# A mixture-of-experts loop whose 2 MB weight blocks come over one queue: the blocks of the second matrix are issued from ScalarE instead

## The chip, the cores and the metric

The kernel runs on one core of a Trainium2 chip. The metric is the device time of one execution in microseconds (us). The median of three executions of the kernel before is 1500.68 us (1499.49 to 1815.03). The profiled execution, from which all rows below come, took 1503.03 us, of which its span is 1501.1 us.

## What is computed

One layer of a hybrid backbone on 256 latent and 256 context tokens of width 1024, in float32: a token mixer (three kinds of scans), then a mixture of 32 experts of which each token uses four. This case is about the mixture:

```python
for e in range(N_EXPERTS):                       # 32
    gu = t @ p['moe_w_gu'][e] + p['moe_b_gu'][e]     # (256, 1024) @ (1024, 2048)
    glu, lin = jnp.split(gu, 2, axis=-1)
    glu = jnp.minimum(glu, SWIGLU_LIMIT)
    lin = jnp.clip(lin, -SWIGLU_LIMIT, SWIGLU_LIMIT)
    act = glu * jax.nn.sigmoid(SWIGLU_ALPHA * glu) * (lin + 1.0)
    y = y + gates[:, e:e + 1] * (act @ p['moe_w_down'][e] + p['moe_b_down'][e])   # (256, 1024) @ (1024, 1024)
```

The kernel computes, for each expert, only the (at most 64) tokens that chose it; an expert chosen by more gets an extra round behind the 32. All weights of all 32 experts are read whatever the routing: 32 x 6 blocks of 2 MB.

## The kernel before, in words

**Blocks and ring.** An expert's first matrix (`moe_w_gu`) comes as four blocks of 2 MB, its second (`moe_w_down`) as two. The text calls them U0 to U3 and D4, D5. All go through a ring of eight slots (`RING = 8`), filled in the order U0 U1 U2 U3 D4 D5 of expert 0, then of expert 1 and so on: block q goes to slot q mod 8. `ring_full[r]` counts landings in slot r, `ring_free[r]` how often TensorE is through with it. The loops are unrolled over groups of four experts (`GROUP`), since after four experts (24 blocks) the slots repeat.

**SyncE (SP) before.** SyncE issues every block in that order (line 605, in `load_slot`), each behind a wait for its slot (lines 610 and 629). The first eight have no earlier use of the slot to wait for: U0 to U3 of expert 0 come as soon as the mixer's output is there, D4 and D5 wait for the four slots in which `w_out` lay (`slot_free`), and the next two for steps of the router stage (`h2_ready`, the copies hk0 and hk1).

**TensorE (PE).** `expert(m, i, ...)` does, in this order: `up` (U0 to U3: two chunks of rows, k, to a block, four matmuls of 128x512 to a chunk, with a scatter of the expert before and the transposes `select_back` after chunk 0 and the bias after chunk 3), a second part of the scatter, `turn` of half 0, `gather` for an expert to come, `turn` of half 1, `down` (D4, then D5). A matmul in float32 is two instructions in the trace: 16 to an up block, 32 to `down`. `up` waits for `ring_full` of a block and gives its slot free behind its last matmul.

**VectorE (DVE).** When U3 is done (it waits for that slot's `ring_free`), the clamps L1707 and L1708, L1711, and L1714, which multiplies by the sigmoid; then the same for the second half. TensorE's turn (L2499) waits for L1714. Later L1734 takes down's result.

**ScalarE (ACT).** `expert` there: `copy_selT` (L1062, behind `select_back`), `sigmoid_half` 0 and 1 (L1052, each behind L1707's `glu_ready`), `copy_actT` (L1057) and `copy_gathered` (L1047). In the loop over groups (`Fori`) the first expert has two table loads (`ACT_TABLE_LOAD`), one ahead of L1062's copy and one ahead of the first L1052, since the table of the sigmoid is another than the copy's. The last group, written out behind the loop, has none ahead of its sigmoids.

Nothing in this kernel orders the blocks on the DMA engines except the order in which SyncE issues them: one queue, first in, first out.

Of the kernel before, what the change touches and what calls it, by code (L numbers as in the profile page):

```python
# [17 lines left out]
E, TOPK, FF, SLOTS = 32, 4, 1024, 64  # L18
EXTRA = L * TOPK // SLOTS
WORDS = 53152  # L20
RING = 8
PER = 6
GROUP = 4
# [214 lines left out]
def hybrid_block(nc, a):  # L238

    with ExitStack() as ctx:  # L240
# [198 lines left out]
        def pair(name, n=1024):  # L439

            g = R.group(name)
            return PS[:, 2 * g:2 * g + 2, :].rearrange("p a b -> p (a b)")[:, 0:n]
# [81 lines left out]
        def ring_at(m, i, s):  # L524

            q = PER * i + s
            return q % RING, m * 3 + q // RING

        def extra_at(j, s):

            return s, j + E * PER // RING
# [3 lines left out]
        @block.sync  # L535
        def _(sp):
            def slot_wait(kind, n):

                for s, count in before[kind, n]:
                    sp.wait_ge(slot_free[s], count)  # L540

            sp.dma_start(Cb(C_ID), a["consts"][:, 0:P]).then_inc(ident_in, 16)
            sp.dma_start(xtok[:, 0:2, :], a["ctx"][0].rearrange("(i p) d -> p i d", p=P)).then_inc(x_in, 16)
            sp.dma_start(xtok[:, 2:4, :], a["x"][0].rearrange("(i p) d -> p i d", p=P)).then_inc(x_in, 16)

            def load_ada(n):
                s = place["ada", n][0]
                slot_wait("ada", n)
                sp.dma_start(slots[s], w_ada_k[n % 8, :, n // 8 * 2048:n // 8 * 2048 + 2048]).then_inc(slot_full[s], 16)

            sp.dma_start(Cb(1, C_N - 1), a["consts"][:, P:]).then_inc(consts_in, 16)
            sp.wait_ge(rows_in, 16 * N_ROWS)
            for n in range(8):
                load_ada(n)


            sp.wait_ge(zeroed, 1)

            def mats(dst, src):
                sp.dma_start(dst, src).then_inc(mats_in, 16)  # L560

            def spread(dst, src):

                mats(dst, src.partition_broadcast(P))

            for d in range(2):
                spread(w0b[:, 256 * d:256 * d + 256], a["rw_w0"][0, d, :])
                spread(gbb[:, P * d:P * d + P], a["gla_gate_b"][0, d, :])
                spread(dtb[:, 8 * d:8 * d + 8], a["ssd_dt_bias"][0, d, :])
                spread(alog[:, 8 * d:8 * d + 8], a["ssd_a_log"][0, d, :])  # L570
                mats(W2A[32 * d:32 * d + 32, 256 * d:256 * d + 256], a["rw_w2"][0, d])
                mats(gwb[16 * d:16 * d + 16, P * d:P * d + P], a["gla_gate_w"][0, d])
            spread(rbb, a["router_b"][0])
            spread(dall, a["ssd_d"][0])
            mats(W2A[64:96, 0:256], a["rw_a2"][0])
            mats(g2w[0:64, :], a["rw_g2"][0])
            mats(dtw[:, :, :], a["w_in"][0].rearrange("(k p) c -> p k c", p=P)[:, :, DT0:DT0 + 16])
            mats(rtw[:, :, :], a["router_w"][0].rearrange("(k p) c -> p k c", p=P))

            for s, _, kind, n in loads[8:]:  # L580
                if kind == "in":
                    c0, w, _ = W_GROUPS[n]
                    slot_wait("in", n)
                    sp.dma_start(w_in_tile(n), w_in_k[:, :, c0:c0 + w]).then_inc(slot_full[s], 16)
                elif kind == "ada":
                    load_ada(n)
            sp.wait_ge(gla_done, 1)
            for n in range(4):
                if n == 2:
                    sp.wait_ge(rw_in, 8)  # L590
                s = place["out", n][0]
                slot_wait("out", n)
                sp.dma_start(slots[s].rearrange("p (k c) -> p k c", k=2), w_out_k[:, 2 * n:2 * n + 2, :])\
                    .then_inc(slot_full[s], 16)


            sp.wait_ge(cat_ready, 1)
            for x in range(2):
                sp.dma_start(bgrow[32 * x:32 * x + E, :], a["moe_b_gu"][0, :, FF * x:FF * x + FF]).then_inc(late_in, 16)
            sp.dma_start(bdn[0:E, 0:D], a["moe_b_down"][0]).then_inc(late_in, 16)  # L600

            def load_slot(r, e, s):

                src = gu_k[bass.ds(e, 1), s, :, :] if s < 4 else dn_k[bass.ds(e, 1), s - 4, :, :]
                sp.dma_start(ring[r], src.rearrange("a p c -> p (a c)")).then_inc(ring_full[r], 16)

            for q in range(PER * GROUP):
                r, used = q % RING, q // RING
                if used:
                    sp.wait_ge(ring_free[r], used)  # L610
                elif r in (4, 5):
                    for x in range(2):
                        sp.wait_ge(slot_free[2 * r - 6 + x], base[2 * r - 6 + x])
                elif r == 6:
                    R.emptied(sp, "n2")
                    sp.wait_ge(h2_ready, 1)
                    R.emptied(sp, "xk0")
                    R.emptied(sp, "xk1")
                elif r == 7:
                    R.arrived(sp, "m5")  # L620
                    R.arrived(sp, "fg")
                    R.emptied(sp, "hk0")
                    R.emptied(sp, "hk1")
                load_slot(r, q // PER, q % PER)
            with sp.Fori(1, E // GROUP) as m:
                for i in range(GROUP):
                    for s in range(PER):
                        r, used = ring_at(m, i, s)
                        sp.wait_ge(ring_free[r], used)
                        load_slot(r, m * GROUP + i, s)  # L630

            R.emptied(sp, "lst")
            extra = sp.value_load(ints[0:1, 0:1], min_val=0, max_val=EXTRA)
            with sp.If(extra > 0):
                with sp.Fori(0, extra) as j:
                    e = sp.value_load(ints[0:1, bass.ds(j + 8, 1)], min_val=0, max_val=E - 1)
                    for s in range(PER):
                        r, used = extra_at(j, s)
                        sp.wait_ge(ring_free[r], used)
                        load_slot(r, e, s)  # L640
            for i in range(2):
                sp.wait_ge(out_ready, i + 1)
                sp.dma_start(a["out"][0, i * P:(i + 1) * P, :], xk[:, i, :]).then_inc(out_done, 16)
            sp.wait_ge(out_done, 32)
# [99 lines left out]
        def _(act):  # L744
# [269 lines left out]
            R.drained("m5", act.copy(m5r[0:E, :], pair("m5")[0:E, :]))  # L1014
            R.arrived(act, "fg")
            R.drained("fg", act.copy(fgr, pair("fg")))
            R.emptied(act, "n2")
            act.activation(r2, r2, ACT.Sqrt).then_inc(root_ready, 1)
            act.activation(small[:, 44:45], small[:, 12:13], ACT.Exp)  # L1019
# [29 lines left out]
            def sigmoid_half(n, half):  # L1049

                act.wait_ge(glu_ready, n * 2 + (half + 1))
                act.activation(sgm[:, 256 * half:256 * half + 256], glu[:, 256 * half:256 * half + 256], ACT.Sigmoid, scale=ALPHA).then_inc(sig_ready, 1)  # L1052
# [6 lines left out]
            def copy_selT(n, buffer):  # L1059

                act.wait_ge(selT_done, n + 1)
                act.copy(SW[:, buffer, :], PS[:, 3, 0:L]).then_inc(sw_ready, 1)  # L1062

            def expert(m, i, gathers):

                n = m * GROUP + i
                copy_selT(n, i % 2)
                sigmoid_half(n, 0)
                sigmoid_half(n, 1)
                copy_actT(n, 0, PS[:, 3, 0:256])  # L1070
                if gathers:
                    copy_gathered(i % 2, n + 3, (i // 2 + 1) % 2, 2)
                copy_actT(n, 1, PS[:, 0, 0:256])

            def extra_expert(j):

                n = j + E
                act.wait_ge(gathered, j + (E + 1))
                act.copy(hg[:, 0, 0:4, :].rearrange("p k t -> p (k t)"), PS[:, 2, :]).then_inc(hg_ready, 1)
                copy_selT(n, 1)  # L1080
                sigmoid_half(n, 0)
                sigmoid_half(n, 1)
                copy_actT(n, 0, PS[:, 3, 0:256])
                copy_actT(n, 1, PS[:, 0, 0:256])
# [4 lines left out]
                for i in range(GROUP):  # L1089
                    expert(m, i, True)  # L1090
            for i in range(GROUP):
                expert(E // GROUP - 1, i, i < 2)
            R.emptied(act, "lst")
            extra = act.value_load(ints[0:1, 0:1], min_val=0, max_val=EXTRA)
            with act.If(extra > 0):
                with act.Fori(0, extra) as j:
                    extra_expert(j)
            act.activation(small[:, 44:45], small[:, 12:13], ACT.Sqrt)
            for i in range(2):
                act.wait_ge(scattered, i + 1)  # L1100
# [1510 lines left out]
```

## Time and profile before

| | |
|---|---|
| median of 3 executions | 1500.68 us |
| profiled execution | 1503.03 us, span 1501.1 us |
| TensorE busy | 1336.3 us (89%) |
| VectorE, ScalarE, GpSimd busy | 411.4, 227.3, 53.1 us |
| DMA queue q1 (all from SyncE) | 451.38 MB, 72.2% of 16 engines' span |
| DMA queue q10 (from ScalarE) | 276 packets, 0.08 MB |
| read from HBM | 450.40 MB |

The span has two parts. Up to about 575 us the mixer and the router run. From there to the end the 32 experts run, TensorE is in the nines in every one of the 40 slices, and the DMA engines move 424 to 429 GB/s in nearly all of them. In a row of the timeline the number ahead is the start in us, the second the duration, and the brackets say how long the engine was idle before it and what ended that. In a DMA row the last number is the time from issue to landing.

### The profile page before, as it was taken

To read this page: it belongs to the slowest core of one execution; us is meant where nothing else is said; L and a number is where in the kernel's file an instruction comes from. 1 tells how busy PE (TensorE), PEld (TensorE's weight loads), DVE (VectorE), ACT (ScalarE), POOL (GpSimd) and SP (SyncE) were. 2 spreads that over 40 slices of the span, in tenths; PEclk is the share of its full clock that TensorE was granted. 3 is DMA by queue.
4 is the path that set the end of the run, shared out by engine and by line. 5 is a ranking of instruction groups with operands and counts; after the bars stand their busy time and mean duration, and the time that the engine had idled before them with its cause. 6 is when DMAs were issued, how large, how long until landed. Compare 5 with 4: busy or idle time off the path is not lost.

```text
span 1501.1 us, 21678 instructions
## 1 busy us (share of the span) xinstructions
PE 1336.3 (89%) x9148; PEld 639.8 (43%) x9148; DVE 411.4 (27%) x959; ACT 227.3 (15%) x426; POOL 53.1 (4%) x84
## 2 busy tenths in 40 slices
PE   4999998644888979999999999999999999998997
PEld 2545546423878874333333333333333333333332
DVE  0131135487454442112112112112112112111211
ACT  2122103332232131001001001001001001000101
POOL 0000000043121000000000000000000000000000
PEclk8999999866899979999999999999999999999999
DMA  8536510000101197999999999999999999999995
GB/s 331 189 138 226 202 68 0 1 0 19 40 3 59 47 380 290 424 428 426 427 426 428 428 427 428 427 428 427 427 427 429 428 427 427 428 428 426 428 426 234
DMA packets 44886, 452.44 MB, mean 301 GB/s; under 512 B 6998, under 2 KB 10036, under 8 KB 17044
## 3 DMA queue, kind: packets, MB, share of 16 engines
q1 hardware_dynamic: 44544, 451.38, 72.2%
q8 instruction: 53, 0.87, 0.2%
q10 hardware_dynamic: 276, 0.08, 0.0%
q14 instruction: 13, 0.11, 0.0%
HBM read 450.40 MB, written 1.05 MB: 301 GB/s over the span
## 4 chain that ended last, share of the span: by engine, by line
PE 43%; DMA 16%; DVE 3%; issue 1%; ACT 1%; DVEq 0%; SPq 0%
PE PS L1786 42%; DMA arena<-in_moe_w_gu 16%; PE PS L2499 1%; DVE arena L1708 1%; DVE arena L1711 1%; DVE arena L1714 1%; PE PS L2490 1%; ACT arena L1026 0%; DVE arena L1707 0%; DVE arena L1614 0%; ACT arena L1101 0%; DVE arena L1779 0%; ACT L1019 0%; DVEq L240 0%; DVE arena L1643 0%
## 5 line engine op out<-in xcount | busy, mean ns | idle before, releaser
L1786 PE MATMUL PS<-arena 128*64 128x512 f32 (+11 forms) x8746 | 1282.1, 425 | 113.5 <-DVE arena L1410 23.7
L1786 PEld LDWEIGHTS PS<-arena 128*64 128x64 f32 (+7 forms) x8746 | 593.2, 152 | 750.5 <-issue 599.9
L1707 DVE TENSOR_SCALAR arena<-PS 128x256 f32<-128x256 f32 x64 | 38.6, 602 | 522.3 <-PE PS L1786 522.3
L1052 ACT ACTIVATE arena<-arena 128x256 f32<-128x256 f32 x64 | 26.7, 418 | 491.1 <-DVE arena L1707 491.1
L1734 DVE TENSOR_TENSOR arena<-PS,arena 128x512 f32<-128x512 f32 x32 | 22.1, 692 | 219.3 <-PE PS L1786 219.3
L1062 ACT COPY arena<-PS 128x256 f32<-128x256 f32 x32 | 11.9, 373 | 288.7 <-PE PS L2490 288.7
L2499 PE MATMUL PS<-arena 128*128 128x128 f32 x128 | 26.2, 286 | 29.9 <-DVE arena L1714 29.9
L1205 DVE SCALAR_TENSOR_TENSOR arena<-PS,arena 128x255 f32<-128x255 f32 (+5 forms) x68 | 32.7, 481 | 41.8 <-ACT arena L820 39.5
L1708 DVE TENSOR_SCALAR arena<-PS 128x256 f32<-128x256 f32 x64 | 39.0, 610 | 0.0
L2499 PEld LDWEIGHTS PS<-arena 128*128 128x128 f32 x128 | 14.5, 141 | 56.1 <-DVE arena L1714 30.8
L1711 DVE SCALAR_TENSOR_TENSOR arena<-arena 128x256 f32<-128x256 f32 x64 | 27.3, 426 | 2.8
L1714 DVE TENSOR_TENSOR arena<-arena 128x256 f32<-128x256 f32 x64 | 27.3, 426 | 2.2
L1047 ACT COPY arena<-PS 128x512 f32<-128x512 f32 x32 | 18.8, 587 | 46.1 <-PE PS L1786 46.1
L1057 ACT COPY arena<-PS 128x256 f32<-128x256 f32 x64 | 23.5, 368 | 5.6 <-PE PS L2499 5.6
L1477 DVE TENSOR_TENSOR arena<-arena,PS 128x256 f32<-128x256 f32 x40 | 16.9, 421 | 24.4 <-PE PS L1786 23.7
L1690 DVE TENSOR_SCALAR arena<-arena 128x128 f32<-128x128 f32 x64 | 19.1, 341 | 0.0
L1463 DVE COPY arena<-PS 128x512 f32<-128x512 f32 x16 | 11.0, 689 | 27.6 <-PE PS L1786 27.6
L2490 PEld LDWEIGHTS PS<-arena 128*128 128x128 f32 x64 | 6.5, 141 | 24.3 <-issue 24.3
L983 ACT COPY arena<-PS 128x512 f32<-128x512 f32 x16 | 9.4, 587 | 41.3 <-PE PS L1786 41.3
L674 POOL TENSOR_TENSOR arena<-arena 128x128 f32<-128x128 f32 x8 | 3.5, 443 | 320.6 <-DVE arena L1328 309.6
L1300 DVE TENSOR_SCALAR arena<-PS,arena 128x256 f32<-128x256 f32 (+1 forms) x32 | 11.1, 410 | 11.3 <-ACT arena L891 11.2
L2490 PE MATMUL PS<-arena 128*128 128x128 f32 x64 | 14.0, 301 | 0.0
(276 smaller groups left out, 464.0 us busy)
## 6 DMA issues: line engine op xcount, KB each, us to landing
arena<-in_moe_w_gu SPq DMA_DIRECT2D x128, 2048.0 KB, 26.5
arena<-in_moe_w_down SPq DMA_DIRECT2D x64, 2048.0 KB, 29.0
arena<-in_w_ada SPq DMA_DIRECT2D x24, 1024.0 KB, 7.4
arena<-in_w_in SPq DMA_DIRECT2D x5, 2048.0 KB, 9.2
arena<-in_w_out SPq DMA_DIRECT2D x4, 1024.0 KB, 6.7
arena<-in_w_in SPq DMA_DIRECT2D x1, 1664.0 KB, 6.9
arena<-in_consts SPq DMA_DIRECT2D x1, 1536.0 KB, 11.0
arena<-in_w_in SPq DMA_DIRECT2D x1, 1152.0 KB, 5.6
```

Of the source, the lines that this page charges most:

```text
L1052: act.activation(sgm[:, 256 * half:256 * half + 256], glu[:, 256 * half:256 * half + 256], ACT.Sigmoid, scale=ALPHA).then_inc(sig_ready, 1)
L1057: act.copy(actT[:, 2 * half:2 * half + 2].rearrange("p a b c -> p (a b c)"), src).then_inc(actT_ready, 1)
L1205: ins = dve.scalar_tensor_tensor(out=d_, in0=s_, scalar=wgt, in1=d_, op0=ALU.mult, op1=ALU.add)
L1690: ins = dve.tensor_scalar(selw[:, i, :, :], slot_ids.unsqueeze(1).to_broadcast([P, 2, SLOTS]), pos(i), gates[:, i, bass.ds(e, 1)], ALU.is_ ...
L1707: dve.tensor_scalar(by_rest(glu), of_half(0), LIMIT, None, ALU.min).then_inc(glu_ready, 1)
L1708: dve.tensor_scalar(by_rest(lin), of_half(1), LIMIT, -LIMIT, ALU.min, ALU.max).then_inc(moe_vec, 1)
L1711: dve.scalar_tensor_tensor(out=lin[:, cols], in0=lin[:, cols], scalar=1.0, in1=glu[:, cols], op0=ALU.add, op1=ALU.mult).then_inc(moe_vec, 1)
L1714: dve.tensor_tensor(act_[:, cols], lin[:, cols], sgm[:, cols], ALU.mult).then_inc(act_ready, 1)
L1734: dve.tensor_tensor(ye, PS[:, 3, :], m5h, ALU.mult).then_inc(ye_ready, 1)
L1786: ins = pe.matmul(out, lhsT, rhs, start=start, stop=stop, skip_group_check=skip)
L2490: ins = pe.transpose(PS[:, 3, t * P:t * P + P], selw[:, t, :, :].rearrange("p a b -> p (a b)"), ident)
L2499: ins = pe.transpose(dst[:, c * P:c * P + P], act_[:, (2 * half + c) * P:(2 * half + c + 1) * P], ident)
```

## The change

`load_slot` on SyncE becomes `load_up`, which issues U0 to U3 only. D4 and D5 are issued by ScalarE (`load_down`): those of expert 0 behind the copies of m5 and fg, ahead of the n2 step; those of expert n+1 inside expert n, behind `copy_selT` and ahead of the sigmoids. Slots, sizes, semaphores and the waits for them stay.

```diff
-            def load_slot(r, e, s):
+            def load_up(r, e, s):
-                src = gu_k[bass.ds(e, 1), s, :, :] if s < 4 else dn_k[bass.ds(e, 1), s - 4, :, :]
-                sp.dma_start(ring[r], src.rearrange("a p c -> p (a c)")).then_inc(ring_full[r], 16)
+                sp.dma_start(ring[r], gu_k[bass.ds(e, 1), s, :, :].rearrange("a p c -> p (a c)")).then_inc(ring_full[r], 16)
...
             with sp.Fori(1, E // GROUP) as m:
                 for i in range(GROUP):
-                    for s in range(PER):
+                    for s in range(4):
                         r, used = ring_at(m, i, s)
                         sp.wait_ge(ring_free[r], used)
-                        load_slot(r, m * GROUP + i, s)
+                        load_up(r, m * GROUP + i, s)
...
             R.drained("fg", act.copy(fgr, pair("fg")))
+            def load_down(r, e, s):
+                act.dma_start(ring[r], dn_k[bass.ds(e, 1), s - 4, :, :].rearrange("a p c -> p (a c)")).then_inc(ring_full[r], 16)
+            for s in (4, 5):
+                for x in range(2):
+                    act.wait_ge(slot_free[2 * s - 6 + x], base[2 * s - 6 + x])
+                load_down(s, 0, s)
             R.emptied(act, "n2")
...
-            def expert(m, i, gathers):
+            def load_next(m, i):
+                for s in (4, 5):
+                    r, used = ring_at(m + (i + 1) // GROUP, (i + 1) % GROUP, s)
+                    act.wait_ge(ring_free[r], used)
+                    load_down(r, m * GROUP + (i + 1), s)
+            def expert(m, i, gathers, more=True):
                 n = m * GROUP + i
                 copy_selT(n, i % 2)
+                if more:
+                    load_next(m, i)
                 sigmoid_half(n, 0)
```

The last expert issues nothing (`more` is false). The extra rounds are changed in the same way.

SyncE's program at the first blocks of the ring, before (the brackets name the semaphores that a row waits for):

```order
L605 DMA arena<-in_moe_w_gu 128x4096 x4
L605 DMA arena<-in_moe_w_down 128x4096 [waits slot_free3,slot_free2]
L605 DMA arena<-in_moe_w_down 128x4096 [waits slot_free5,slot_free4]
L605 DMA arena<-in_moe_w_gu 128x4096 [waits pair_free0,pair_free1,h2_ready,pair_free3]
L605 DMA arena<-in_moe_w_gu 128x4096 [waits pair_free3,pair_free0,pair_full2,pair_full1]
L605 DMA arena<-in_moe_w_gu 128x4096 [waits ring_free0]
L605 DMA arena<-in_moe_w_gu 128x4096 [waits ring_free1]
L605 DMA arena<-in_moe_w_down 128x4096 [waits ring_free2]
L605 DMA arena<-in_moe_w_down 128x4096 [waits ring_free3]
```

and in the change:

```order
L604 DMA arena<-in_moe_w_gu 128x4096 x4
L604 DMA arena<-in_moe_w_gu 128x4096 [waits pair_free0,pair_free1,h2_ready,pair_free3]
L604 DMA arena<-in_moe_w_gu 128x4096 [waits pair_free3,pair_free0,pair_full2,pair_full1]
L604 DMA arena<-in_moe_w_gu 128x4096 [waits ring_free0]
L604 DMA arena<-in_moe_w_gu 128x4096 [waits ring_free1]
L604 DMA arena<-in_moe_w_gu 128x4096 [waits ring_free4]
L604 DMA arena<-in_moe_w_gu 128x4096 [waits ring_free5]
```

The four rows of the second matrix have left SyncE's program; the others keep their waits.

ScalarE's program at the first expert of the loop over groups, before (L1062 is copy_selT, L1052 the sigmoid, ISA and REGISTER_ALU work on addresses and counts):

```order
L1062 ACT_TABLE_LOAD
L1062 COPY arena<-PS 128x256 [waits selT_done]
L1051 ISA
L1052 ACT_TABLE_LOAD
L1052 ACTIVATE arena<-arena 128x256 [waits glu_ready]
L1051 REGISTER_ALU
L1052 ACTIVATE arena<-arena 128x256 [waits glu_ready]
L1057 COPY arena<-PS 128x256 [waits actT_done]
```

and in the change, where L1069 is copy_selT, L1018 the DMA and L1059 the sigmoid:

```order
L1069 ACT_TABLE_LOAD
L1069 COPY arena<-PS 128x256 [waits selT_done]
L1075 ISA
L1018 ISA [waits ring_free2]
L1018 DMA arena<-in_moe_w_down 128x4096
L1018 ISA [waits ring_free3]
L1018 DMA arena<-in_moe_w_down 128x4096
L1058 ISA
L1059 ACT_TABLE_LOAD
L1059 ACTIVATE arena<-arena 128x256 [waits glu_ready]
L1058 REGISTER_ALU
L1059 ACTIVATE arena<-arena 128x256 [waits glu_ready]
```

Two waits and two issues now stand between the copy and the sigmoid, and the sigmoid's table load stands behind them.

## Rows read from the trace of the kernel before

**Rows 1.** Page, part 2: GB/s in 40 slices of 37.5 us

```profile
GB/s 331 189 138 226 202 68 0 1 0 19 40 3 59 47 380 290 424 428 426 427 426 428 428 427 428 427 428 427 427 427 429 428 427 427 428 428 426 428 426 234
```

**Rows 2.** Chain that ended last, pieces: start us, us, what

```profile
704.83 1.79 PE PS L1786 x16
...
732.92 1.79 PE PS L1786 x16
...
1087.27 32.71 DMA arena<-in_moe_w_gu
...
1143.91 34.91 DMA arena<-in_moe_w_gu
...
1202.75 34.90 DMA arena<-in_moe_w_gu
```

**Rows 3.** Stretches of all engines: us, PE, PEld, DVE, ACT, POOL busy, PEclk, DMA share, GB/s

```profile
525.00:537.00 12.00, 11.43 (x68) 10.27 (x68) 5.61 (x9) 3.02 (x4) 0.00 (x0) 1.00 1.01 433
577.90:1479.70 901.80, 858.08 (x4228) 308.71 (x4224) 167.96 (x431) 87.90 (x198) 0.00 (x0) 1.00 1.01 427
```

**Rows 4.** Timeline of all engines, 1200 to 1232 us

```profile
1202.75 0.33 SPq L605 DMA_DIRECT2D arena<-in_moe_w_gu  x1
1207.35 5.09 SPq L605 DMA_DIRECT2D arena<-in_moe_w_down  x2
1208.28 4.71 PE L1786 MATMUL PS<-arena 128*64 128x512 f32 x20 [1.10 <-DMA arena<-in_moe_w_gu]
1216.39 9.86 PE L1786 MATMUL PS<-arena 128*64 128x512 f32 x44
1220.23 8.76 SPq L605 DMA_DIRECT2D arena<-in_moe_w_gu  x3
```

**Rows 5.** Last block's issue, and the last two blocks' KB and time to landing

```profile
1448.83 0.33 SPq L605 DMA_DIRECT2D arena<-in_moe_w_down  x1
arena<-in_moe_w_down SPq DMA_DIRECT2D x1, 2048.0 KB, 35.4
```

**Rows 6.** Chain that ended last, 1460 us to the end

```profile
1439.48 34.91 DMA arena<-in_moe_w_gu
1474.43 3.68 PE PS L1786 x16
...
1483.57 7.04 PE PS L1786 x32
...
1496.71 1.19 DVEq L240
```

**Rows 7.** Timeline, 1084 to 1150 us: where activation starts on DVE and ACT

```profile
1119.89 4.29 SPq L605 DMA_DIRECT2D arena<-in_moe_w_down  x2
1123.73 0.60 DVE L1707 TENSOR_SCALAR arena<-PS 128x256 f32<-128x256 f32 x1 [16.32 <-PE PS L1786]
1124.36 0.42 ACT L1052 ACTIVATE arena<-arena 128x256 f32<-128x256 f32 x1 [14.14 <-DVE arena L1707]
1125.27 0.43 DVE L1714 TENSOR_TENSOR arena<-arena 128x256 f32<-128x256 f32 x1
1138.86 1.28 ACT L1052 ACT_TABLE_LOAD   x1
```

**Rows 8.** Timeline of the DMA issues and ScalarE: first blocks, longest early issue from ScalarE

```profile
2.48 0.72 ACTq L760 DMA_DIRECT2D arena<-in_c  x1
...
532.63 0.81 SPq L605 DMA_DIRECT2D arena<-in_moe_w_down  x2
536.05 1.00 ACT L1016 COPY arena<-PS 128x1024 f32<-128x1024 f32 x1
540.48 0.42 ACT L1018 ACTIVATE arena<-arena 128x256 f32<-128x256 f32 x1 [3.43 <-DVE arena L1616]
```

**Rows 9.** DMA issues, 595 to 597 us: KB, us to landing; and 595:596 GB/s

```profile
arena<-in_moe_w_gu SPq DMA_DIRECT2D x1, 2048.0 KB, 9.1
595.00:596.00 1.00, 1.00 (x7) 0.28 (x4) 0.00 (x0) 0.00 (x0) 0.00 (x0) 1.00 0.80 344
```

**Rows 10.** DMA queues, 4 to 5 and 6 to 7 us: packets, MB, share

```profile
q1 hardware_dynamic: 97, 0.40, 97.9%
...
q1 hardware_dynamic: 90, 0.37, 91.0%
q10 hardware_dynamic: 67, 0.03, 9.7%
```

**Rows 11.** DMA packets, 1185 to 1215 us

```profile
DMA packets 880, 12.85 MB, mean 428 GB/s; under 512 B 96, under 2 KB 96, under 8 KB 96
```

More of the change, by code:

```diff
@@ L600, in _ @@
             sp.dma_start(bdn[0:E, 0:D], a["moe_b_down"][0]).then_inc(late_in, 16)
-            def load_slot(r, e, s):
-                src = gu_k[bass.ds(e, 1), s, :, :] if s < 4 else dn_k[bass.ds(e, 1), s - 4, :, :]
-                sp.dma_start(ring[r], src.rearrange("a p c -> p (a c)")).then_inc(ring_full[r], 16)
[L607 to L624, printed above, removed]
+            def load_up(r, e, s):
+                sp.dma_start(ring[r], gu_k[bass.ds(e, 1), s, :, :].rearrange("a p c -> p (a c)")).then_inc(ring_full[r], 16)
+            for e in range(GROUP):
+                for s in range(4):
+                    q = e * PER + s
+                    r, used = q % RING, q // RING
+                    if used:
+                        sp.wait_ge(ring_free[r], used)
+                    elif r == 6:
+                        R.emptied(sp, "n2")
+                        sp.wait_ge(h2_ready, 1)
+                        R.emptied(sp, "xk0")
+                        R.emptied(sp, "xk1")
+                    elif r == 7:
+                        R.arrived(sp, "m5")
+                        R.arrived(sp, "fg")
+                        R.emptied(sp, "hk0")
+                        R.emptied(sp, "hk1")
+                    load_up(r, e, s)
             with sp.Fori(1, E // GROUP) as m:
                 for i in range(GROUP):
-                    for s in range(PER):
+                    for s in range(4):
                         r, used = ring_at(m, i, s)
                         sp.wait_ge(ring_free[r], used)
-                        load_slot(r, m * GROUP + i, s)
+                        load_up(r, m * GROUP + i, s)
             R.emptied(sp, "lst")
@@ L636, in _ @@
                     e = sp.value_load(ints[0:1, bass.ds(j + 8, 1)], min_val=0, max_val=E - 1)
-                    for s in range(PER):
+                    for s in range(4):
                         r, used = extra_at(j, s)
                         sp.wait_ge(ring_free[r], used)
-                        load_slot(r, e, s)
+                        load_up(r, e, s)
             for i in range(2):
@@ L1073, in expert, with extra_expert @@
                 copy_actT(n, 1, PS[:, 0, 0:256])
-            def extra_expert(j):
+            def extra_expert(j, e):
                 n = j + E
@@ L1080, in extra_expert @@
                 copy_selT(n, 1)
+                for s in (4, 5):
+                    r, used = extra_at(j, s)
+                    act.wait_ge(ring_free[r], used)
+                    load_down(r, e, s)
                 sigmoid_half(n, 0)
@@ L1091, in _ @@
             for i in range(GROUP):
-                expert(E // GROUP - 1, i, i < 2)
+                expert(E // GROUP - 1, i, i < 2, i < GROUP - 1)
             R.emptied(act, "lst")
@@ L1096, in _ @@
                 with act.Fori(0, extra) as j:
-                    extra_expert(j)
+                    e = act.value_load(ints[0:1, bass.ds(j + 8, 1)], min_val=0, max_val=E - 1)
+                    extra_expert(j, e)
             act.activation(small[:, 44:45], small[:, 12:13], ACT.Sqrt)
```

## The prediction

> **What bounds the kernel now.** I read the page's slices first. From the seventeenth slice on the core reads 424 to 429 GB/s, slice after slice [rows 1]; the stretch table says 427 GB/s from 577.9 to 1479.7 us with the DMA engines busy all the time [rows 3]. A block of 2.097 MB at 427 GB/s is 4.91 us, an expert of six blocks 29.4 us. The chain of waits tells who sets the pace. Early in the loop it runs over TensorE alone, one expert in 28.09 us (732.92 minus 704.83), and from 1087 us over block landings, two experts in 58.84 us (1202.75 minus 1143.91), that is 29.42 each [rows 2]. TensorE could go 1.3 us per expert faster than the blocks come; it does so only while it eats the stock in the ring. So the end is: the moment at which the DMA engines get going without a pause (577.9 us), plus the bytes left, plus what TensorE does after the landing it needs. Moving the other engines by less than 1.3 us per expert changes nothing; the DMA rate, a pause of the DMA engines and the tail do.
>
> **The tail.** The last U3 is issued at 1439.48 and lands 34.91 us later, at 1474.4; TensorE starts its last up block at 1474.43 and the kernel ends 26.7 us later, at 1501.1 [rows 6]. The last D5 is issued at 1448.83 and lands 35.4 later, at 1484.2 [rows 5], 9.8 us (two blocks) behind U3. Its use is in the second half of the 32 matmuls that start at 1483.57, from 1487.1 on [rows 6]: nobody waits for it. Today the second matrix comes last and is also needed last, and that hides its two block times under activation and turn.
>
> **What the change moves.** Same 192 blocks, same slots, same waits. SyncE loses 64 issues of 0.33 us [rows 4], ScalarE gains them. SyncE's time bought nothing before, since it waits between its issues, so its saving is worth 0. What is new is that D blocks stand in another queue than the up blocks, and no longer behind them.
>
> (a) *Order on the DMA engines.* Let t = 0 be the landing of U3 of expert n (1208.28 in [rows 4]). Up to seven blocks stand in the queue by then (34.9 us from issue to landing over 4.91). U0 to U3 of expert n+1 are all issued (the last at t = -5.5). D4 of n+1 is issued at -0.9 and D5 at +3.8 (1207.35 + 5.09 - 0.33 = 1212.11) [rows 4]. In one queue they land at 34.3 and 39.2. ScalarE issues them at the same events. If the DMA engines take the two queues in turn, the order of landing is U0, D4, U1, D5, U2, U3 at 4.9, 9.8, 14.7, 19.6, 24.5 and 29.4. TensorE wants them thus: U3's matmuls and the activation end and `down` starts at +8.1 (1216.39) and ends 32 x 0.22 = 7.0 later, U0 starts at 15.2, U1 at 20.0, U2 at 24.4, U3 at 27.9 (my count: 3.5 us per block, 1.3 for scatter and transposes, 0.9 for the bias). The new order meets these within 0.1 us, except U3, on which TensorE waited before as well. The period stays 29.4 us.
>
> (b) *Does the ring run dry?* D blocks now lie longer in their slots. At t = 3.8 six blocks are issued and 0.8 gone. The next issue, U0 of n+2 into D4's slot, comes at 1220.23, t = 11.9 [rows 4]: by then 11.9/4.91 = 2.4 are gone and 3.6 left. The next three follow up to t = 24. The engines never empty, so 0. What would take this cover away is a TensorE later by 3.6 blocks, 17 us.
>
> (c) *The tail.* For expert 31 the same order holds, and now U3 is the last of all bytes. The bytes end when they ended before, so U3 lands at 1484.2 instead of 1474.4, and the 26.7 us behind it follow unshortened: **+9.8 us**. Bounds: 0, if the blocks still landed in order of issue; 9.8, if both D blocks pass it. Since D4 and D5 are issued 25 us before U3's turn comes, even a much smaller share for ScalarE's queue lets them pass. I take 9.8.
>
> (d) *ScalarE in the loop.* Its wait for `ring_free` of U3's slot ends when DVE starts L1707 (1123.73); SyncE's issue at that event ended at 1124.18 (1119.89 + 4.29). The sigmoid starts at 1124.36 and L1714, which needs it, at 1125.27, 0.49 us after the sigmoid's end [rows 7]. Between bounds of 0.33 and 0.72 us (the longest early issue from ScalarE [rows 8]) for an issue, all of it is hidden: 0. But in the first expert of each group the sigmoid's table load of 1.28 us [rows 7], which ran in idle time, now follows the issue: 1124.18 + 1.28 = 1125.46 in place of 1124.36, 1.1 late, of which 0.49 is slack, so 0.6 to 1.0 us per four experts; I take 0.7. Under the 1.3 us per expert that TensorE has to spare, it costs nothing, save where the DMA engines have no stock: at expert 0. There U0 of expert 2 was issued at 595.90 and landed after 9.1 us [rows 9], at 605.0, though D5 of expert 1 had landed at 598.6: 6.4 us for a block, so the queue was about empty, and 595 to 596 shows 344 GB/s [rows 9]. This issue comes **0.7 us** later, and all behind it.
>
> (e) *Start of the ring.* D4 and D5 of expert 0 were issued at 532.63; ScalarE reaches them when its copy at 536.05 is over, at 537.1. The first four blocks keep the engines busy till 541 (520.4 + 19.6 and a start of 1 us). The two issues end by 538 and ScalarE's next work, at 540.48, waited for DVE [rows 8]. 0; bound 3.4 us of cover.
>
> **Sum.** 1503.03 + 9.8 + 0.7 = 1513.5 for the profiled execution. It lies 2.3 us over the median, so by the median 1500.7 + 10.5 = 1511.2; I forecast 1511.
>
> **Can two queues cost or give rate?** The only stretch with both queues busy is the start. From 6 to 7 us 67 small packets from ScalarE ran between SyncE's, and took 9.7% of 16 engine-us: 23 ns each, their own bytes included. SyncE's packets moved 0.37 MB in 91.0% there and 0.40 MB in 97.9% with the queue alone [rows 10], the same rate within rounding. So a change of queue costs 0 to 23 ns. As to gains, one queue alone has shown 433 GB/s over 12 us against 427 [rows 3]; twelve microseconds at a start are a weak bound, but it is the only one: 1.4% of 904 us, 12.7 us.
>
> **Rivals.** *A, order of issue holds* (ScalarE's blocks wait their turn behind those already queued, or U3 is served first): the tail is as before, 1503.7, by the median 1501.4. For it: nothing but that the start's packets are small. Against: these ran between SyncE's within the same microsecond. The Trainium skill ("DMA: Bandwidth & Descriptors", section "Issuing engines are not separate DMA queues") says that issuing from several engines saves only issue time; taken as the whole story it is this rival, by that sentence about 0 gained or lost. Chance 0.13.
>
> *B, slower than before by over 2%: switching.* An expert has 128 packets of data per block (784 in the 6.1 blocks of [rows 11], 96 small ones aside), 8 per DMA engine. If the queues alternate packet by packet, four of six blocks are interleaved: 32 packets at 23 ns, 0.74 us per expert, 22.8 us over 31 experts. 1513.5 + 22.8 = 1536.3, by the median 1534, 2.2% over before. It decides from (30 - 10.5)/904 = 2.2% of rate, at under 418 GB/s. Against it: SyncE's rate did not fall at the start. The skill's same page (section "Queues, rings and completion order") says a DMA engine takes queues in turn but drains a packet of some 9 to 17 descriptors before it switches; by that the switches would be a few per expert and B would shrink to some 3 us, an estimate from that page; the order of landing in (a) would be the same. No run here shows it yet. Chance 0.12, half of it past 2%.
>
> *C, two queues raise the rate* to 433 GB/s: 1513.5 - 12.7 = 1500.8, by the median 1498.5. For it only that row; engines already busy at share 1.01 speak against. Chance 0.06, over 2% faster 0.01 to 0.02.
>
> *D, ScalarE late by more than 1.3 us per expert*, if an issue of 2 MB held it over 2 us: for each microsecond beyond, 32 us. Issues of this size took SyncE 0.33. Chance 0.03.
>
> **Chances and range.** The forecast (1508 to 1515 by itself) has 0.66. The range of 1499 to 1524 takes in A, C and the milder half of B. "Within 2%", about what a measurement of this kernel can tell from no change, is 1470.7 to 1530.7: faster 0.02, same 0.90, slower 0.08.
>
> **What would show it.** Right: D blocks land after some 10 to 16 us instead of 35, U3 of the last expert is the last to land, some 26.7 us before the end, 427 GB/s throughout, and in the chain TensorE begins to wait for blocks earlier than 1087 us (9.8 us of stock gone at 1.3 per expert, seven experts). Wrong: D blocks still at 30 us (A), under 420 GB/s in the slices (B), a pause of the DMA engines (b), or L1714 waiting for the sigmoid in every expert (D).

## The result, and the profile after

The change takes 1512.45 us (median of 11 executions, 1507.34 to 1665.8) against 1501.78 us for the kernel before on the same chip (median of 11, 1494.78 to 1815.03). The one long execution of each (1665.8 and 1815.03 us) is left out of the ratio. The ratio is 1.0072, with a 95% interval of 1.0052 to 1.0092: slower by 0.7%, within 2%. The forecast was 1511 us, with 1499 to 1524 as its range and 0.90 for "within 2%".

The profiled execution of the change has a span of 1506.9 us, 5.8 us over that of before. One thing must be known to read this and what follows: the part ahead of the experts differs by some microseconds from one execution to the next. TensorE's first matmul of expert 0 started at 572.12 us in the profile of before and at 565.86 in that of the change; over the ten profiles of this study that start lies between 563.6 and 573.8. So I compare the **loop time**, from that matmul to the end of the span: 929.0 us before (1501.1 - 572.12), **941.0 us in the change** (1506.9 - 565.86), 12.1 us more. The medians say 10.7. Each loop time is that of one execution; how far such a number can be trusted is shown under experiments 6 to 8.

The page's line of GB/s in 40 slices of 37.7 us, of the kernel after:

```profile
GB/s 329 207 134 210 240 29 0 1 0 57 3 54 9 142 316 340 422 426 427 427 426 428 428 428 428 428 427 428 427 428 427 428 428 428 428 428 428 426 426 114
```

As in [rows 1], the DMA engines move 422 to 428 GB/s slice after slice from the seventeenth to the last but one. Two stretches more exactly (columns as in [rows 3]), of the kernel after:

```profile
571.67:631.67 60.00, 59.00 (x290) 21.14 (x286) 10.77 (x28) 6.06 (x13) 0.00 (x0) 1.00 0.99 410
631.67:1411.67 780.00, 736.13 (x3616) 266.37 (x3610) 145.57 (x376) 78.52 (x174) 0.00 (x0) 1.00 1.01 428
```

and the same two in the kernel before:

```profile
577.90:637.90 60.00, 59.84 (x292) 21.36 (x290) 10.79 (x28) 4.77 (x12) 0.00 (x0) 1.00 1.00 422
637.90:1417.90 780.00, 740.50 (x3654) 266.56 (x3652) 145.64 (x376) 78.54 (x174) 0.00 (x0) 1.00 1.01 427
```

Over 780 us two queues move 428 GB/s where one moves 427: no rate is lost to switching between them and none is gained. In the first 60 us behind the first refill, 410 stand against 422, which is 60 x 12/422 = 1.7 us of transfer.

Now the order of landing. These are single blocks around the last matmuls of one expert in the middle of the loop, each as its issue (start us behind "to") and its time from issue to landing, of the kernel after: U1 and U3 from SyncE, D4 and D5 from ScalarE.

```profile
L604 SPq DMA_DIRECT2D arena<-in_moe_w_gu x1: 333/333/333, 1200.0 to 1200.0; - x1
DMA to landing us min/median/max: 30.5/30.5/30.5
...
L604 SPq DMA_DIRECT2D arena<-in_moe_w_gu x1: 333/333/333, 1208.4 to 1208.4; - x1
DMA to landing us min/median/max: 34.9/34.9/34.9
...
L1018 ACTq DMA_DIRECT2D arena<-in_moe_w_down x1: 339/339/339, 1213.0 to 1213.0; - x1
DMA to landing us min/median/max: 14.0/14.0/14.0
...
L1018 ACTq DMA_DIRECT2D arena<-in_moe_w_down x1: 339/339/339, 1217.8 to 1217.8; - x1
DMA to landing us min/median/max: 19.0/19.0/19.0
```

With t = 0 at the landing of U3 of the expert before (1213.9), D4 lands at 1227.0, t = 13.1; U1 at 1230.5, t = 16.6; D5 at 1236.8, t = 22.9; U3, issued ahead of both D blocks, last, at 1243.3, t = 29.4. U0 (24.1 from 1196.5) landed at 6.7 and U2 (33.4 from 1205.0) at 24.5. The order is U0, D4, U1, D5, U2, U3. In the kernel before it was U0 to U3, then D4, D5, D5 after 35.4 us [rows 5].

The end of the chain, of the kernel after (start us, us, what):

```profile
1444.93 35.27 DMA arena<-in_moe_w_gu
1480.24 3.68 PE PS L1807 x16
1486.05 0.44 PE PS L2520 x2
1486.48 2.68 PE PS L1807 x24
...
1489.38 7.04 PE PS L1807 x32
```

From U3's landing (1480.2) to the end (1506.9) are 26.7 us, as in [rows 6]. Before, U3 landed 902.3 us behind the first matmul of expert 0 (1474.4 - 572.1), now 914.3 us behind it. The whole loss has arisen by then. Two blocks are 9.8 us of it.

The rest of the 12.1 us starts at expert 0. The timeline there, of the kernel after:

```profile
581.67 0.35 ACTq L1018 DMA_DIRECT2D arena<-in_moe_w_down  x1
...
582.12 1.28 ACT L1059 ACT_TABLE_LOAD   x1 [13.54 <-PE PS L1807]
583.41 0.42 ACT L1059 ACTIVATE arena<-arena 128x256 f32<-128x256 f32 x1
583.93 0.43 DVE L1735 TENSOR_TENSOR arena<-arena 128x256 f32<-128x256 f32 x1 [0.88 <-ACT arena L1059]
```

DVE stands idle for 0.88 us until the sigmoid is done, which stands behind the table load, which stands behind the issue. From the end of up to the start of `down` took 4.49 us in the kernel before (587.79 to 592.28) and 5.34 us now (581.52 to 586.86): 0.85 us late. The table of waits (us in total, times, longest) has it seven times, once per group but the last:

```profile
DVE arena L1735 <- ACT arena L1059: 6.0, 7, 0.9
```

In the other experts the issues stay hidden, as (d) of the prediction had it: this is one of them, of the kernel after.

```profile
1213.00 5.09 ACTq L1018 DMA_DIRECT2D arena<-in_moe_w_down  x2
1217.63 0.61 DVE L1728 TENSOR_SCALAR arena<-PS 128x256 f32<-128x256 f32 x1 [17.11 <-PE PS L1807]
1218.27 0.42 ACT L1059 ACTIVATE arena<-arena 128x256 f32<-128x256 f32 x1 [14.93 <-DVE arena L1728]
```

The second issue ends at 1218.09 and the sigmoid starts 0.64 us behind DVE's L1728, as before (0.63 in [rows 7]).

### The profile page after: what moved, and what is told of

Read it like the earlier page. It is cut to its first block, busy times and chain, and to the rows that moved or that the text cites. A ratio compares the mean times of both kernels' runs of the same rounds, so it can differ in the third digit from the quotient of the medians.

```text
span 1506.9 us, 21702 instructions
## 1 busy us (share of the span) xinstructions
PE 1334.5 (89%) x9148; PEld 637.5 (42%) x9148; DVE 411.3 (27%) x959; ACT 227.0 (15%) x427; POOL 53.1 (4%) x84
## 4 chain that ended last, share of the span: by engine, by line
PE 39%; DMA 21%; DVE 3%; issue 1%; ACT 1%; ACTq 0%; DVEq 0%; SPq 0%
PE PS L1807 38%; DMA arena<-in_moe_w_gu 21%; PE PS L2520 1%; DVE arena L1729 1%; DVE arena L1735 1%; PE PS L2511 1%; DVE arena L1732 0%; ACT arena L1033 0%; DVE arena L1635 0%; DVE arena L1728 0%; ACT arena L1122 0%; ACT arena L1059 0%; ACTq L1018 0%; DVE arena L1800 0%; ACT L1026 0%
## 5 line engine op out<-in xcount | busy, mean ns | idle before, releaser
L1728 DVE TENSOR_SCALAR arena<-PS 128x256 f32<-128x256 f32 x64 | 38.6, 603 | 525.2 <-PE PS L1807 525.2
L1059 ACT ACTIVATE arena<-arena 128x256 f32<-128x256 f32 x64 | 26.7, 417 | 401.2 <-DVE arena L1728 401.1
L2520 PE MATMUL PS<-arena 128*128 128x128 f32 x128 | 26.7, 291 | 35.7 <-DVE arena L1735 35.7
L1069 ACT COPY arena<-PS 128x256 f32<-128x256 f32 x32 | 11.9, 373 | 289.7 <-PE PS L2511 289.7
L1321 DVE TENSOR_SCALAR arena<-PS,arena 128x256 f32<-128x256 f32 (+1 forms) x32 | 11.1, 411 | 11.3 <-ACT arena L889 11.2
## 6 DMA issues: line engine op xcount, KB each, us to landing
arena<-in_consts SPq DMA_DIRECT2D x1, 1536.0 KB, 10.8
```

The costliest lines, as they stand in the source:

```text
L1728: dve.tensor_scalar(by_rest(glu), of_half(0), LIMIT, None, ALU.min).then_inc(glu_ready, 1)
L2520: ins = pe.transpose(dst[:, c * P:c * P + P], act_[:, (2 * half + c) * P:(2 * half + c + 1) * P], ident)
```

## The experiments

All of them are versions of the change or of the kernel before, each timed beside the kernel before on the same chip. The tables' loop time is from the profiled execution.

**1. Only the last expert's D blocks back on SyncE.**

```diff
-            with sp.Fori(1, E // GROUP) as m:
-                for i in range(GROUP):
-                    for s in range(4):
+            with sp.Fori(1, E // GROUP - 1) as m:
+                load_group(m)
+            load_group(E // GROUP - 1, last=True)
...
+                    for s in range(PER if last and i == GROUP - 1 else 4):
...
-                expert(E // GROUP - 1, i, i < 2, i < GROUP - 1)
+                expert(E // GROUP - 1, i, i < 2, i < GROUP - 2)
```

> The change, with one difference: D4 and D5 of the last expert (31) are issued by SyncE behind U3 of that expert, all others by ScalarE. Loop time is counted from TensorE's first matmul of expert 0 to the end of the span, since the part ahead of it differs by some us from execution to execution: 929.0 us before, 941.0 in the change. Theory (the tail: U3 of the last expert lands two blocks later): the 9.8 us come back whole, loop time 931.2, ratio to before about 1.001, U3 of expert 31 lands two blocks ahead of D5. Rival (two queues cost something in every expert: switching, or ScalarE's waits): nothing or little comes back, loop time 939 to 941, ratio about 1.007.

Measured: ratio 1.0071 (1.0057 to 1.0086), loop time 939.8 us. Only 1.2 of the 9.8 us came back; by the numbers written down, the rival won. The end of its chain shows why (kernel of experiment 1):

```profile
1421.72 36.07 DMA arena<-in_moe_w_gu
1457.84 3.68 PE PS L1815 x16
...
1477.15 13.36 PE PS L1815 x64
```

TensorE waited for U3 of expert 30, which landed at 1457.8, and for no block of expert 31: its 64 matmuls from 1477.15 on run through U3 without a break. Expert 30 was already late: its turn comes 11.2 us later behind the first matmul of expert 0 than in the kernel before (889.9 for 878.7 us). TensorE's own work from U3 to U3 takes 29.0 us there, so it is at U3 of expert 31 at 1486.8 and not earlier, whatever has landed. The theory "the last U3 lands late" was too narrow. What the change makes is a **standing lag**: once TensorE waits for blocks it runs two blocks behind where it ran before, in every expert, and can win back only its own wait of 1.3 us in each. That is a new theory with numbers of its own; experiments 6 to 8 test it.

**2. The table load ahead of the issues.**

```diff
                 copy_selT(n, i % 2)
+                if i == 0:
+                    act.activation(small[:, 44:45], small[:, 12:13], ACT.Sigmoid)
                 if more:
                     load_next(m, i)
```

> The change, with a one-column sigmoid behind copy_selT in the first expert of each group, so that the table load of 1.28 us runs while ScalarE is idle and no longer behind the two issues. Theory: loop time 941.0 minus the 0.8 us by which expert 0 is late in the change, and minus what the DMA engines pause more in the first 60 us of the loop (410 GB/s for 422 before, 1.7 us), so 939.2; the 9.8 us stay; ratio to before about 1.006. Rival (the table load is absorbed and the 2.2 us beside the tail are the price of two queues): loop time stays at 941.0.

Measured: loop time 939.0 us (expected 939.2, rival 941.0); ratio 1.0077 (1.0061 to 1.0093), where about 1.006 was expected. The ratio doesn't show the gain: two microseconds are at the edge of what these ratios can tell. The trace does, and it shows where the gain lies. The first 60 us behind the first refill (kernel of experiment 2):

```profile
576.98:636.98 60.00, 59.84 (x292) 21.34 (x290) 10.80 (x28) 4.77 (x12) 0.00 (x0) 1.00 1.00 422
```

With the table load out of the way two queues move 422 GB/s there, as one queue did before. So the 410 of the change came from the exposed table load and not from the second queue, and it makes up the 2 us that the two blocks leave open.

**3. Both.**

> Both together: the last expert's D blocks from SyncE, and the table load ahead. Theory: nothing of the loss is left, loop time 929 to 929.5 as before, ratio 1.000. Rival (two queues cost by themselves): loop time 931 or more.

Measured: loop time 938.2 us, ratio 1.0058 (1.0043 to 1.0073). The 929 of my theory failed with experiment 1, for the same reason: -1.2 and -2.0 us give 937.8.

**4. One queue, only the last expert's order changed.** The kernel before, with

```diff
-                    for s in range(PER):
+                    for s in (0, 1, 4, 5, 2, 3) if last and i == GROUP - 1 else range(PER):
```

> The kernel before, all blocks from SyncE's one queue; only for the last expert the order of issue is U0 U1 D4 D5 U2 U3. Theory (only the place of U3 in the order of landing counts, not the queue or the engine): loop time 929.0 + 9.8 = 938.8, ratio about 1.0065, U3 lands 26.7 us before the end. Rival (the loss has to do with ScalarE or the second queue): loop time 929, ratio 1.000.

Measured: loop time 939.8 us (expected 938.8; the rival said 929), ratio 1.0069 (1.0051 to 1.0087). The rows of its TensorE at the end:

```profile
1437.68 4.71 PE L1791 MATMUL PS<-arena 128*64 128x512 f32 x20 [1.25 <-DMA arena<-in_moe_w_gu]
1471.99 10.55 PE L1791 MATMUL PS<-arena 128*64 128x512 f32 x36 [8.69 <-DMA arena<-in_moe_w_gu]
```

Here the whole delay arises in one expert, as a wait of 8.7 us for U2. ScalarE issues nothing in this kernel and there is no second queue: moving two blocks ahead of U2 and U3 of the last expert alone costs 10.8 us. The price is the order of landing, whoever issues. It is 1.0 us over two blocks, since TensorE waits for U2 and not for U3 as I had expected: U2's matmuls and what lies between them take 5.8 us (10.55 - 4.71), longer than the 4.9 us in which U3 lands behind U2.

**5. The issues behind the sigmoids.**

```diff
-                if more:
-                    load_next(m, i)
                 sigmoid_half(n, 0)
                 sigmoid_half(n, 1)
+                if more:
+                    load_next(m, i)
```

> The change, with the two issues behind both sigmoids of the expert instead of ahead of them: the table load lies in idle time again, but the D blocks are issued some 3 us (D5) and 6.5 us (D4) later. Theory (at expert 0 the DMA engines have no stock: what is issued late there is a pause and lasts to the end; later issues are covered by three to five blocks in the queues): U2 and U3 of expert 1 keep them busy for 9.8 us from the first refill, D4 follows after 14.5 + 1.6 us, so the pause is about 4.6 to 6 us and takes the place of the 1.5 us pause of before: loop time 929.0 + 9.8 + 3 to 4.5 = 942 to 943.5. Rival (the ring always has stock, and freeing ScalarE helps): loop time 939, as with the table load moved ahead.

Measured: loop time 943.1 us, inside the 942 to 943.5 of the theory; the rival said 939. Ratio 1.0083 (1.0066 to 1.01). The issues of expert 1's D blocks, and the DMA engines around them (kernel of experiment 5):

```profile
590.61 0.86 ACTq L1018 DMA_DIRECT2D arena<-in_moe_w_down  x2
...
583.00:593.00 10.00, 9.84 (x52) 4.57 (x50) 4.33 (x11) 2.05 (x5) 0.00 (x0) 1.00 0.67 244
598.00:618.00 20.00, 20.00 (x92) 6.24 (x90) 2.73 (x6) 0.79 (x2) 0.00 (x0) 1.00 1.01 431
```

244 GB/s in those 10 us for some 427 is a pause of 4.3 us. It is in the end time: 943.1 us against the 939.0 of experiment 2, in which the table load is hidden too and the blocks are issued ahead of the sigmoids. The same lateness in every later expert costs nothing: TensorE's turn comes 4.2 us later than in experiment 2 at expert 19 and 4.1 us later at expert 31.

**6 to 8. More experts in the old order.** D blocks of the last four (6) or the last eight experts (7, 8) are issued by SyncE behind U3; experiment 8 has the early table load of experiment 2 too. `load_group` issues four or six blocks per expert from SyncE. With k groups:

```diff
+            with sp.Fori(1, E // GROUP - k) as m:
+                load_group(m, 4)
+            for m in range(E // GROUP - k, E // GROUP):
+                load_group(m, PER)
...
+            for m in range(E // GROUP - 1 - k, E // GROUP - 1):
+                for i in range(GROUP):
+                    expert(m, i, True, m == E // GROUP - 1 - k and i < GROUP - 1)
...
-                expert(E // GROUP - 1, i, i < 2, i < GROUP - 1)
+                expert(E // GROUP - 1, i, i < 2, False)
```

More groups are thus written out on ScalarE as well, and the exposed table load is gone in them: DVE waits for it 6 times in experiment 6 and 5 times in experiment 7, for 7 in the change.

> The change, with the D blocks of the last four experts (28 to 31) issued by SyncE in the old order, those of experts 0 to 27 by ScalarE. Loop time is counted as above: 929.0 us before, 941.0 in the change, 939.8 with only the last expert in the old order. Theory (a standing lag: from the moment at which TensorE waits for blocks it runs two blocks, 9.8 us, later in the change than before, and it can only catch up by leaving out its wait of 1.3 us per expert): four experts and the start of the first give back 4 to 5 times 1.3, so loop time 941.0 - 5.3 to 6.5 = 934.5 to 936. Rival 1 (only the order within the last expert matters, and something else held the first of these experiments back): 939 to 940 as there. Rival 2 (a price of two queues in every expert, in proportion): 4 of 32, 939.5.

> The same with the last eight experts (24 to 31) in the old order. Theory of the standing lag: eight times 1.3 is more than 9.8, so the lag is gone before the end, the last U3 lands two blocks ahead of the last D5 and TensorE waits for it again; what is left is the 2.2 us of the start: loop time 941.0 - 9.8 = 931.2, ratio to before about 1.0015. Rival 1: 939 to 940. Rival 2 (8 of 32 of 12): 938.

> The last eight experts in the old order and the sigmoid's table load ahead of the issues in the first expert of each group. Theory: nothing of the loss is left, loop time 929 to 930, ratio 1.000 to 1.001, though 24 of 32 experts still have their D blocks from ScalarE. Rival (a rest is the price of two queues at the start of the loop): loop time stays at 931.

| experts in the old order | loop time, us | expected | ratio (95% interval) |
|---|---|---|---|
| 0 (the change) | 941.0 | | 1.0072 (1.0052 to 1.0092) |
| last 1 | 939.8 | 931.2 (the first theory) | 1.0071 (1.0057 to 1.0086) |
| last 4 | 936.6 | 934.5 to 936 | 1.0065 (1.005 to 1.008) |
| last 8 | 930.7 | 931.2 | 1.0037 (1.0023 to 1.0051) |
| last 8, table load ahead | 929.3 | 929 to 930 | 1.0001 (0.999 to 1.0012) |
| 32 (the kernel before) | 929.0 | | 1 |

Against the change 1.2, 4.4 and 10.3 us come back for one, four and eight experts. The two rivals (only the last expert, or a price in proportion) said 939 to 940 and 938 for the last eight. Experiment 6 missed its range by 0.6 us. At expert 0, where the DMA engines have no stock, the granted clock fell to 0.50 in its profile (the last section comes back to this): the first 60 us moved 402 GB/s, against 411 in experiment 1, which is 1.3 us.

The traces show the lag itself. This is the time from TensorE's first matmul of expert 0 to its first turn of expert n, for the kernel before, and how much later it is in the others (us):

| expert n | 11 | 15 | 19 | 23 | 27 | 31 |
|---|---|---|---|---|---|---|
| before | 328.7 | 441.0 | 553.7 | 671.4 | 789.1 | 908.1 |
| the change | +5.8 | +7.0 | +11.9 | +11.9 | +11.9 | +12.1 |
| experiment 2 (table load ahead) | 0.0 | +5.1 | +10.0 | +10.0 | +10.0 | +10.1 |
| experiment 4 (one queue, last expert) | 0.0 | 0.0 | -0.1 | -0.1 | -0.1 | +10.8 |
| experiment 6 (last 4) | +4.0 | +8.6 | +13.5 | +13.5 | +13.5 | +7.7 |
| experiment 7 (last 8) | +4.2 | +6.7 | +11.6 | +11.6 | +6.2 | +1.7 |
| experiment 8 (last 8, table load ahead) | +0.2 | +5.0 | +10.0 | +10.0 | +4.5 | +0.3 |

The entries for expert 31, less the start of the loop, are these rows of the chain (before, and the kernels of experiments 2 and 8; that of the change stands above, at 1486.05):

```profile
1480.23 0.44 PE PS L2499 x2
...
1489.41 0.44 PE PS L2522 x2
...
1472.04 0.44 PE PS L2534 x2
```

In experiment 2 TensorE keeps pace with the kernel before up to expert 11. From there the new order makes it wait while the kernel before still eats its stock, so the lag grows by some 1.25 us per expert (5.1 us from expert 11 to 15, 4.9 from 15 to 19). At 10.0 us, two blocks, it stops growing, since the kernel before now waits too, and it stands to the end. In experiment 8 the same lag is worked off from expert 24 on, 5.4 us in the first four experts. The two kernels differ only in who issues the last eight experts' D blocks and in how ScalarE's last groups are written out, and they are 9.8 us apart at the end (918.2 and 908.4). Single profiles can carry this: up to expert 11 the kernels with no exposed table load whose D blocks come in time (before, 2, 3, 4, 8) agree within 0.2 us.

In experiment 7 TensorE waits for the last U3 again, issued 34.6 us before (kernel of experiment 7):

```profile
1211.47 34.90 DMA arena<-in_moe_w_gu
...
1438.62 34.56 DMA arena<-in_moe_w_gu
1473.18 0.04 issue
1473.22 3.68 PE PS L1819 x16
```

Between these two DMA steps the chain holds no landing: the one at 1246.4 is the last that stopped TensorE before the one at 1473.2. That is the catching up. Experiment 8 is as fast as the kernel before, with 24 of 32 experts' D blocks still issued from ScalarE, so two queues cost nothing by themselves (0.3 us of loop time, a ratio of 0.999 to 1.0012). The ratios of experiments 6 and 7 (1.0065 and 1.0037) lie above what their loop times give (7.6 and 1.7 us, 1.0051 and 1.0011), and between 7 and 8 the medians differ by 4.6 us, the loop times by 1.4; the front part was not what I changed there, and I can't say where the rest of it comes from.

None of these versions beats both kernels.

## Why the prediction was right, point by point

**The bound.** Right: 427 to 428 GB/s throughout, a period of 29.42 us behind the transition, and an end set by the bytes and the tail. That 1511 came within 1.5 us of the median of 1512.45 is in part luck: the loop time rose by 12.1 us for the 10.5 of the sum, the medians by 10.7.

**(a) Order of landing.** Right in order, and for U0 to U3 within 2 us. The D blocks land at t = 13.1 and 22.9 for 9.8 and 19.6, 3.3 us late. They are two blocks' time (9.8 us) apart, as if each had half the rate; by that D4 was taken up at t = 3.3, 4.2 us behind its issue, where I had let it start at once. This is an estimate from the landing times, and the reason for the 4.2 us is not shown. TensorE asks for the blocks later, so it changed nothing.

**(b) The ring doesn't run dry.** Right in the steady part. Experiment 5 shows that this stock is missing at one place only, the first refill.

**(c) The tail, +9.8 us.** The size is right (9.8 us between experiments 2 and 8, 10.0 for the standing lag, 10.8 for the reorder alone in experiment 4), and so is the cause, the order of landing. What the text missed is that this is not a matter of expert 31. I worked out the steady order in (a), with U3 two blocks later in each expert, and then charged the price at the end only. Experiment 1 showed the difference: curing expert 31 alone gives back 1.2 us.

**(d) ScalarE.** Right: 0.34 to 0.35 us for an issue, hidden wherever no table load follows; the table load exposed once per group, 0.85 us at expert 0 for the 0.7 taken. Too small in the sum: the 0.7 us taken for the start of the loop measured 2.0, the loop time that moving the table load took off. The DMA engines' pause (410 for 422 GB/s, 1.7 us) grew by more than TensorE's lateness of 0.85 us; why is not shown.

**(e) Start of the ring.** Right. ScalarE issued expert 0's two blocks at 529.57 and 530.03, which is 535.8 and 536.3 on the clock of before (6.26 us later), 1.3 us ahead of the 537.1 that I took: the issues did not wait for the end of the copy in front of them, which ran from 529.84 to 530.84.

**Rivals.** A (order of issue holds) fell with the landing times. B (switching costs rate) and C (two queues give rate) fell with 428 against 427 GB/s; the upper bound of 23 ns per switch from [rows 10] would have shown as 2.5% of that rate. The Trainium skill ("DMA: Bandwidth & Descriptors", section "Queues, rings and completion order") has the queues served in turn; the landing order agrees: D4, issued 16.5 us behind U0 and 4.6 behind U3, landed between U0 and U1. The sentence of the same page that issuing from several engines only saves issue time ("Issuing engines are not separate DMA queues") holds for the rate here, and not for the kernel, which lost 0.7% by it. D (ScalarE late everywhere) fell with the sigmoid's start 0.64 us behind L1728.

**What would show it.** Between 640 and 1450 us D blocks land after 13.6 to 21.6 us, 15.4 in the median; I had written 10 to 16. The first wait of TensorE that is on the chain came earlier than at 1087 us, at the block issued at 975.4, but 3.8 experts earlier counted from expert 0 and not seven (515.2 us behind expert 0's start before, 409.5 now, over 28.1 each). With the table load ahead (experiments 2 and 3) it came 346.8 and 318.7 us behind it, 6.0 and 7.0 experts earlier. So the exposed table loads, and what follows them (below), slow TensorE in the part where it is the bound: it is 5.8 us late at expert 11 in the change, and not at all in experiment 2.

## What to carry to other kernels

A second DMA queue is a change of order before it is anything else: when one queue holds several blocks in stock, blocks issued on another overtake them (here 14 and 19 us to landing beside 24 to 35), and if those are the blocks needed last, everything that is needed first becomes later by their length. A consumer that keeps pace with a saturated stream then runs behind by that much in every turn, and can recover only at the rate of its own slack, so look at what lands last before the end and at how many turns a cure needs. An instruction that is hidden in idle time, such as a table load, is exposed by any wait that is put ahead of it in the same engine's program.

## What the runs showed of the hardware

The exposed table load had a second effect. It lengthens the time between up and turn from 2.0 to 2.9 us at experts 4, 8 and 12. Four small matmuls of the scatter lie in it; behind them TensorE idles for 1.84 us, for 1.02 before. Behind two of the first four such gaps the granted clock fell. These are stretches around and behind the gaps of experts 4 and 8, of the kernel after (the last three columns are PEclk, DMA share, GB/s):

```profile
698.00:700.00 2.00, 0.20 (x1) 0.20 (x2) 1.11 (x3) 1.21 (x2) 0.00 (x0) 0.96 1.04 442
700.00:702.00 2.00, 2.00 (x11) 2.00 (x11) 1.93 (x6) 0.68 (x2) 0.00 (x0) 0.50 0.98 418
...
814.00:816.00 2.00, 1.51 (x13) 1.52 (x14) 1.93 (x5) 0.68 (x2) 0.00 (x0) 0.98 0.98 418
816.00:818.00 2.00, 2.00 (x11) 1.67 (x12) 0.93 (x4) 0.58 (x2) 0.00 (x0) 0.50 1.02 434
```

0.50 is the level of 1.2 GHz, 1.00 that of 2.4 GHz. The 16 gather matmuls behind the first gap took 3.17 us on the chain where they otherwise take 1.79. Behind the gaps of experts 0 and 12 (16 matmuls in 1.78 and 1.79 us) it did not fall, nor in the stretches that I looked at in the kernel before. The other kernels with the exposed table load differ: the 16 matmuls take over 3 us behind expert 0 in experiment 6, after an idle time of only 1.00 us, behind expert 4 in experiment 7, and nowhere in experiment 1. In the kernels without it (before, 2, 3, 4, 5 and 8) no such row is longer than 2.02 us. What decides it the runs don't tell. At experts 4 and 8 it costs the end nothing, since TensorE had 1.3 us per expert to spare; at expert 0 of experiment 6 it cost about 1.3 us.

Issues of 2 MB took ScalarE 0.34 to 0.35 us and SyncE 0.33. And the start of expert 0, ahead of which the profiled program does the same work, spread over 10 us between ten profiles, more than most effects of this study; without a time counted from that point the experiments could not have been told apart.
